# The start of a hybrid decoder step: u of the first 384 tokens from unnormed x, weights issued by two engines

## The reference

```
h = rmsnorm(x, norm1_w)                 # x * rsqrt(mean(x*x) + eps) * w
proj = h @ w_in                         # u, gates, xBC, dt, q, k, v, z
u = proj[..., OFF_U:OFF_Q]              # 512 columns, input of the S5 mixer
bu = einsum('bgph,...', b_bar, u)       # then a scan over time, y, GELU, GLU
gates = sigmoid(proj[..., OFF_GATE:])   # 24 tiles of 128 columns
```

## Time and profile before

| what | value |
|---|---|
| median of three runs | 1685.16 us (1684.84 to 1686.6) |
| span of the profiled execution | 1684.5 us |
| time of the profiled execution beside its span | none given; the span is its measure |
| TensorE busy | 1654.0 us |
| VectorE, ScalarE, GpSimd busy | 966.9, 556.0, 791.2 us |

### The profile page before, as it was taken

The page is one execution under the profiler, slowest core; times in us unless marked ns, Lnnn a source line. Parts: engine busy times, 40 slices in busy tenths (PEclk is TensorE's granted clock), DMA queues, the critical chain, the costliest instruction groups (busy, mean ns, idle before and its releaser), DMA issues. The chain is left out here.

```text
span 1684.5 us, 30884 instructions
## 1 busy us (share of the span) xinstructions
PE 1654.0 (98%) x12241; PEld 1604.7 (95%) x12241; DVE 966.9 (57%) x1642; ACT 556.0 (33%) x1240; POOL 791.2 (47%) x756
## 2 busy tenths in 40 slices
PE   7999999999999999999999999999999999999997
PEld 7999999999999998888899999999999999999997
DVE  6859811406634554778873289666665565744346
ACT  5332121342213332543411154443443333322233
POOL 5483122322221111141322325877777777787774
PEclk9999999999999999999999999999999999999998
DMA  5364363232233234434365431543433344966443
GB/s 209 84 127 133 104 203 98 89 92 91 87 93 103 89 130 134 161 115 140 126 218 191 152 126 42 180 162 145 151 141 141 141 167 165 367 224 267 162 187 103
DMA packets 95805, 245.85 MB, mean 146 GB/s; under 512 B 14369, under 2 KB 42273, under 8 KB 95417
## 3 DMA queue, kind: packets, MB, share of 16 engines
q1 hardware_dynamic: 73824, 174.48, 30.5%
q0 software_dynamic: 10256, 33.59, 6.7%
q10 hardware_dynamic: 11592, 35.96, 6.3%
HBM read 177.11 MB, written 66.65 MB: 145 GB/s over the span
## 5 line engine op out<-in xcount | busy, mean ns | idle before, releaser
L1642 PE MATMUL ps<-HL,WH 128*128 128x384 f32 (+1 forms) x1536 | 507.7, 331 | 4.4 <-DVE HL L691 1.8
L1643 PE MATMUL ps<-HH,WL 128*128 128x384 f32 (+1 forms) x1536 | 497.4, 324 | 0.0
L1644 PE MATMUL ps<-HH,WH 128*128 128x384 f32 (+1 forms) x1536 | 496.3, 323 | 0.0
L1642 PEld LDWEIGHTS ps<-HL,WH 128*128 128x128 f32 x1536 | 289.4, 188 | 15.6 <-issue 9.3
L1643 PEld LDWEIGHTS ps<-HH,WL 128*128 128x128 f32 x1536 | 289.7, 189 | 0.3
L1644 PEld LDWEIGHTS ps<-HH,WH 128*128 128x128 f32 x1536 | 289.6, 189 | 0.0
L1285 POOL TENSOR_TENSOR WL<-WRAW,WH 128x1024 fp32r<-128x1024 f32 x59 | 145.0, 2457 | 243.3 <-DMA WH<-in_w 243.3
L1282 POOL DMA_DIRECT2D WH<-in_w x59 | 34.6, 586 | 354.4 <-PE ps L1644 352.9
L2932 DVE TENSOR_TENSOR X<-X,ps 128x528 f32<-128x528 f32 (+2 forms) x170 | 107.9, 656 | 155.5 <-PE ps L2238 104.6
L2327 ACT ACTIVATE GT<-ps 128x384 f32<-128x384 f32 (+1 forms) x72 | 33.4, 465 | 215.5 <-PE ps L1644 183.5
L2932 DVE TENSOR_TENSOR RB<-RB,ps 128x528 f32<-128x528 f32 x60 | 42.1, 701 | 103.4 <-ACT RB L2847 85.9
(11 more groups left out here) (467 smaller groups left out, 4266.2 us busy)
## 6 DMA issues: line engine op xcount, KB each, us to landing
WRAW<-in_w SPq DMA_DIRECT2D x75, 512.0 KB, 3.4
ffn_scratch<-STG SPq DMA_DIRECT2D x70, 528.0 KB, 3.6
WH<-in_w POOLq DMA_DIRECT2D x62, 512.0 KB, 4.6
SOP<-ffn_scratch SPq DMA_DIRECT2D x36, 528.0 KB, 7.9
gate_scratch<-GT ACTq DMA_DIRECT2D x24, 528.0 KB, 3.2
PX<-gate_scratch ACTq DMA_DIRECT2D x22, 528.0 KB, 4.2
HL<-ffn_scratch SPq DMA_DIRECT2D x22, 528.0 KB, 10.4
RAWB<-in_w SPq DMA_DIRECT2D x10, 1024.0 KB, 6.2
```

The costliest lines, as they stand in the source:

```text
L1642: nc.tensor.matmul(out, wh, rl, start=start, stop=False)
L1643: nc.tensor.matmul(out, wl, rh, start=False, stop=False)
L1644: return nc.tensor.matmul(out, wh, rh, start=False, stop=stop)
```

## The change

In chunk 0, u is computed from x times the norm weight, without the root; the root is multiplied in when VectorE copies u out of the accumulators (evict_first_u_dve). ScalarE and VectorE split this plain x as it lands. Units 0 and 1 come in three transfers for both (256, 256 and 512 columns of each), issued by ScalarE behind the first parameters; their low parts, and those of units 2 to 5, are subtracted by VectorE instead of GpSimd. SyncE issues units 2 and 3 ahead of x of chunk 1, and the bias table after it. The squares of chunk 1 are made first, six on ScalarE and two on VectorE, then those of chunk 0 and 2, each set in buffers of its own. The order of roots is chunk 1, 0, 2, the order of splits 1, 2, 0: the normed h of chunk 0, which the gates need, is split last. Gate 0 is taken in the order of chunks 1, 2, 0; taps begin after gate(1, [0, 1]), and gate(2, [0]) stands ahead of stt_rows(0). ScalarE does gate(2, [0]) ahead of its stt_rows(0) as well, with high_weights(7) still ahead of both. All four stores of u are issued after the last split.

```diff
+    ROOT_ORDER = (1, 0, 2)
+    SPLIT_ORDER = (1, 2, 0)
+    PIECES = [slice(0, 256), slice(256, 512), slice(512, 1024)]
...
+    def x_plain_high_act(k):
+
+        nc.scalar.wait_ge(s_x[k], 16)
+        if k == 0:
+            nc.scalar.wait_ge(s_par, 16)
+        nc.scalar.mul(HH[:, k, 0:384], X0[:, k, 0:384], prm("norm1", k, 1)).then_inc(xp_hi, 1)
+
+    def x_plain_low_dve(k):
+
+        dve = nc.vector
+        dve.wait_ge(xp_hi, k + 1)
+        dve.scalar_tensor_tensor(HL[:, k, 0:384], X0[:, k, 0:384], prm("norm1", k, 1), HH[:, k, 0:384].bitcast(F32),
+                                 ALU.mult, ALU.subtract).then_inc(xp_lo, 1)
...
+    def x_first_squares_act(ks):
+
+        for k in ks:
+            nc.scalar.activation(SQ0[:, k, :], X0[:, k, 0:384], ACT.Square).then_inc(pq_done, 1)
...
+    def x_second_sum_dve():
+
+        dve, pairs = nc.vector, GT[:, 0:768].rearrange("p (k c) -> p k c", c=384)
+        dve.wait_ge(pq_done, 4)
+        dve.tensor_tensor(SQ[:, 0:2], SQ[:, 0:2], SQ[:, 2:4], ALU.add).then_inc(pq_used, 1)
+        dve.wait_ge(s_xc[1], 128)
+        dve.tensor_tensor(pairs, X0[:, 6:8, 384:768], X0[:, 6:8, 384:768], ALU.mult).then_inc(pq_used, 1)
+        dve.wait_ge(pq_used, 2)
+        dve.tensor_tensor(SQ[:, 0:2], SQ[:, 0:2], pairs, ALU.add).then_inc(pq_used, 1)
+        dve.wait_ge(pq_done, SECOND_BY_ACT)
+        dve.wait_ge(pq_used, 3)
+        dve.tensor_tensor(SQ[:, 0:2], SQ[:, 0:2], HF0[:], ALU.add).then_inc(pq_used, 1)
+        dve.wait_ge(pq_used, 4)
+        dve.tensor_tensor(ACC[:, 384:768], SQ[:, 0], SQ[:, 1], ALU.add).then_inc(pq_used, 1)
...
+    def evict_first_u_dve(j):
+
+        dve = nc.vector
+        dve.wait_ge(r0_ok, 1)
+        dve.wait_ge(acc_done[0], j + 1)
+        dve.tensor_tensor(as_steps(UF[:, j, :], 0, 3), as_blocks(u_bank(j, 0), 3), as_blocks(GT[:, 0:384], 3),
+                          ALU.mult).then_inc(acc_free[0], 1)
...
-        x_chunk(0)
+        x_chunk(0, [0])
+        x_chunk(0, [1])
+        x_chunk(0, [2, 3])
+        x_chunk(0, [4, 5, 6, 7])
+        first_weights(2)
+        first_weights(3)
+        x_chunk(1)
         sp.dma_start(HOT[:], io["hot"]).then_inc(s_hot, 16)
         sp.dma_start(RTAB[:], io["rtab"]).then_inc(s_hot, 16)
-        first_weights(0)
-        first_weights(1)
-        first_weights(2)
-        x_chunk(1, range(4))
-        x_chunk(1, range(4, KD))
-        first_weights(3)
         x_chunk(2)
...
-        split_halves()
-        u = 2
+        first_lows_counted()
+        s5_powers()
+        s5_rows()
+        s5_squarings(0)
+        gate_lows_counted()
+        s5_squarings(1)
...
             if n == 0 and j == 2:
-                pe.wait_ge(split_ok, 4)
+                pe.wait_ge(half_ok, 5)
+            elif n == 1 and j == 2:
+                pe.wait_ge(h_lo, KD)
+                pe.wait_ge(r0_ok, 1)
             elif n == 2:
                 pe.wait_ge(acc_free[0], j + 3 if j == 0 else 4)
-                if j == 2:
-                    pe.wait_ge(acc_free[1], 1)
-            elif n == 1 and j == 2:
-                pe.wait_ge(acc_free[0], 1)
-                pe.wait_ge(h_lo, 2 * KD)
             for k in range(KD):
                 if j == 0:
-                    pe.wait_ge(h_lo, KD * n + k + 1)
-                if j == 0 and n == 0 and k in (0, 4):
-                    pe.wait_ge(*((half_ok, 2) if k == 0 else (split_ok, 2)))
+                    pe.wait_ge(*((xp_lo, k + 1) if n == 0 else (h_lo, KD * (n - 1) + k + 1)))
+                if j == 0 and n == 0 and k in (0, 2, 4):
...
+                    pe.wait_ge(half_ok, k // 2 + 1)
...
-        x_first_sums_pe()
-        bias_by_distance(0)
-        bias_by_distance(1)
-        x_spread_pe(0)
         u_pair(0, 0)
-        pe.wait_ge(bias_ev, 2)
-        u_pair(2, 0, {1: lambda: x_sums_pe(1), 3: lambda: x_spread_pe(1)})
-        u_pair(0, 1)
-        u_pair(2, 1, {1: lambda: x_sums_pe(2), 3: lambda: x_spread_pe(2)})
+        u_pair(2, 0, {4: lambda: x_sums_pe(1), 6: lambda: x_spread_pe(1)})
+        u_pair(0, 1, {0: lambda: x_sums_pe(0), 3: lambda: x_spread_pe(0)})
+        u_pair(2, 1, {3: lambda: x_sums_pe(2), 4: lambda: bias_by_distance(0), 5: lambda: x_spread_pe(2),
+                      6: lambda: bias_by_distance(1)})
...
-        gate(0, [0, 1])
+        gate(0, [1, 2])
+        gate(0, [0], lambda n, k: pe.wait_ge(h_lo, 2 * KD + k + 1))
+        gate(1, [0, 1])
         taps(0)
-        gate(0, [2])
         taps(1)
-        gate(1, [0])
+        gate(1, [2])
         taps(2)
-        gate(1, [1])
         taps(3)
-        gate(1, [2])
+        gate(2, [0])
         stt_rows(0)
-        for n in range(3):
-            gate(2, [n])
-            stt_rows(n + 1)
+        stt_rows(1)
+        gate(2, [1])
+        stt_rows(2)
+        gate(2, [2])
+        stt_rows(3)
...
+        for q in range(3):
+            c = PIECES[q]
+            act.dma_start(WRAW[:, :, c], io["w"][0:2, :, c].rearrange("u p n -> p u n")).then_inc(s_piece[q], 16)
...
-        for k in range(0, KD, 2):
-            x_first_square(act, k)
+        x_plain_high_act(0)
+        high_piece(0)
+        x_plain_high_act(1)
+        act.wait_ge(ar_ok, 1)
+        nc.scalar.activation(SF("mag"), SF("ar"), ACT.Exp).then_inc(mag_ok, 1)
+        high_piece(1)
         nc.scalar.activation(SF("unused_root")[:, 0:1], ZERO[:], ACT.Sqrt)
-        high_half(0)
-        x_root_act(0)
-        high_half(1)
-        x_split_act(0, 2)
-        x_squares_act(1, range(2))
-        x_split_act(2, 3)
+        x_plain_high_act(2)
+        x_plain_high_act(3)
+        high_piece(2)
+        for k in range(4, KD):
+            x_plain_high_act(k)
         high_weights(2)
-        x_split_act(3, 4)
-        x_squares_act(1, range(2, 4))
-        x_split_act(4, 5)
         high_weights(3)
-        x_split_act(5, 6)
-        bias_rows(0)
-        x_split_act(6, 7)
-        bias_rows(1)
-        x_split_act(7, 8)
-        x_squares_act(1, range(4, KD))
+        x_squares_act(1, range(SECOND_BY_ACT))
+        x_first_squares_act(range(KD))
         x_root_act(1)
         act.wait_ge(red_ok, 1)
         nc.scalar.activation(SF("sin"), SF("r"), ACT.Sin)
         nc.scalar.activation(SF("cos"), SF("r2"), ACT.Sin).then_inc(sin_ok, 1)
-        x_squares_act(2, range(4))
-        x_split_act(8, 11)
-        evict_u(0, 0)
-        x_split_act(11, 13)
-        evict_u(1, 0)
-        x_split_act(13, 16)
-        x_squares_act(2, range(4, KD))
-        evict_u(2, 0)
-        evict_u(3, 0)
-        x_root_act(2)
+        nc.scalar.activation(SF("unused_root")[:, 0:1], ZERO[:], ACT.Sqrt)
+        for k in range(KD):
+            x_split_act(k, k + 1)
+            if k == 1:
+                x_root_act(0)
+            if k == 5:
+                x_root_copy_act()
+            x_squares_act(2, [k])
         evict_u(0, 1)
         evict_u(1, 1)
-        x_split_act(16, 24)
+        x_root_act(2)
+        x_split_act(8, 10)
+        bias_rows(0)
+        bias_rows(1)
+        x_split_act(10, 12)
         evict_u(2, 1)
+        x_split_act(12, 14)
         evict_u(3, 1)
+        x_split_act(14, 18)
+        high_weights(4)
+        evict_u(0, 2)
+        x_split_act(18, 19)
+        evict_u(1, 2)
+        x_split_act(19, 21)
+        high_weights(5)
+        x_split_act(21, 23)
+        evict_u(2, 2)
+        evict_u(3, 2)
+        x_split_act(23, 24)
         for j in range(4):
-            evict_u(j, 2)
-            if j == 1:
-                high_weights(4)
-                high_weights(5)
+            act.wait_ge(acc_free[0], j + 1)
             act.wait_ge(acc_free[2], j + 1)
             act.dma_start(uscr[j * P:(j + 1) * P, :], UF[:, j, :]).then_inc(s_ust, 16)
...
+        def low_piece(q):
+
+            c = PIECES[q]
+            dve.wait_ge(first_high, q + 1)
+            tt(WL[:, :, c], WRAW[:, :, c], WH[:, :, c].bitcast(F32), ALU.subtract).then_inc(half_ok, 1)
+
+        x_plain_low_dve(0)
+        low_piece(0)
+        x_plain_low_dve(1)
+        low_piece(1)
+        x_plain_low_dve(2)
+        x_plain_low_dve(3)
+        low_piece(2)
+        for k in range(4, KD):
+            x_plain_low_dve(k)
+        for u in (2, 3):
+            dve.wait_ge(first_high, u + 2)
+            tt(high_low(u)[1], WXR[:, u - 2, :], high_low(u)[0].bitcast(F32), ALU.subtract).then_inc(half_ok, 1)
         dve.wait_ge(den_ok, 1)
         nc.vector.reciprocal(SF("den"), SF("den")).then_inc(den_inv, 1)
-        x_split_dve(8, 16)
-        x_add_dve(2, range(KD))
+        x_second_sum_dve()
+        x_first_add_dve(0)
+        x_recip_dve(1)
+        x_first_add_dve(1)
+        x_first_add_dve(2)
+        x_split_dve(0, 3)
+        x_recip_dve(0)
+        x_split_dve(3, 8)
+        x_third_sum_dve()
+        for j in range(2):
+            evict_first_u_dve(j)
         x_recip_dve(2)
-        x_split_dve(16, 24)
+        for j in range(2, 4):
+            evict_first_u_dve(j)
+        x_split_dve(8, 18)
+        dve.wait_ge(first_high, 6)
```

(50 more changed lines are left out.)

178 lines of the change are left out of this document (73 added, 105 removed).

## The result

The changed kernel takes 1693.37 us (median, 1693.05 to 1696.03) against 1685.26 for the kernel before: a ratio of 1.0051, 95% interval 1.0036 to 1.0065. It is slower by 8.1 us, outside the range. The profiled execution took 1693.05 us, with a span of 1691.3, against a span of 1684.5 before.

A forecast was written before the change was run, and what follows sets the result against it. TensorE, busy 98% of the span, was taken as the bound, so only gaps could be saved: 10.5 us at the start, 3.0 left at the first gate, none after unit 7's landing; 1685.2, shifted to 1685.5 us, range 1680.8 to 1689.3.

The forecast's parts named there:

- The chain to the first gate: From the first product to the first gate: start 10.5 us earlier, first gate at 66.2 instead of 69.16, 3.0 left.
- the wait at the sums: At chunk 1's sums: TensorE comes at 22.4 and waits 3.4 us for the squares, until 25.8.
- the sentence on W: VectorE's W passes: 13.8 us uncontended, no term for GpSimd's subtractions, at most 2.1 us.
- The deciding step: Stores of u, then U loads at 78.5: unit 7 lands at 103.0, second transposes at 105.1, the 3.0 us gone.
- Rival A: Shorter chain to the stores of u, gaining 4.5 us to 1680.7; sign: stores out before 67.3; chance 0.29.
- Rival B: Clock at 1.2 GHz from 25.8 on, after the sums: 3.9 us slower, 1689.1; chance 0.22 with other store lateness.
- Rival C: Early start fails, TensorE starts at 12.8, 0.9 us late at chunk 1's sums: 1686.1; within the likeliest case, 0.49.
- the main sum: Start of TensorE at 6.8, first two k at the slow clock to 10.7, first pair ending at 17.2.
- term (d): Waiting at 22.4 may bring back 1.2 GHz: nothing to 2.1 us; small end taken, forecast shifted by 0.3.

The follow-up runs named there:

- e4: Changed kernel plus 36 never-read products of 384 columns on TensorE just ahead of the third gate; 1690.99 us, 1.0035.
- e2: Changed kernel with GpSimd's second set of squarings moved behind unit 6's subtraction and the third set behind unit 7's; 1684.93 us, 0.9997.
- e3: Changed kernel with unit 6's low part subtracted by VectorE instead of GpSimd, GpSimd's order otherwise kept; 1685.98 us, 1.0004.
- e5: Changed kernel with OFF_re and OFF_im set to zero, leaving out six two-operand VectorE passes; 1683.98 us, one execution.
- e8: On top of e2, ScalarE issues the first two weights' three transfers only after x's fourth tile has landed; 1691.64 us, 1.0037.
- e10: On top of e2, every small product of the taps issued twice with the same result; 1698.42 us, 1.0079.
- e9: On top of e6, ScalarE's stt_rows(0) ahead of its gate(2, [0]), and TensorE's taps groups set apart between gate chunks and transposes; 1684.24 us, 0.9992.
- e6: On top of e2, SyncE loads unit 7's weights together with unit 6's, ahead of the loads of U; 1687.35 us, 1.0008.
- e1: Changed kernel with GpSimd's second set of squarings run before it counts the low parts of units 4 and 5; 1696.53 us, 1.0052.
- e11: Kernel before the change, with only GpSimd's first two sets of squarings moved ahead of unit 6's subtraction; 1697.7 us, 1.0066.

## Why the prediction was wrong

**The chain to the first gate** held at every mark: first product 6.8 forecast and 7.06 measured, the wait for the first split of chunk 1 0.85 and 0.80, the ends of chunk 1's two pairs 42.6 and 52.9 against 41.76 and 53.27, first gate 66.2 against 66.37, start of W 71.3 against 71.31. Only the wait at the sums was 1.36 where I had 3.4: TensorE came at 23.4, a microsecond later than thought, and x a little sooner. That was idle either way.

**The step that failed** is the sentence on W: "these subtractions have moved to VectorE, so I take no such term". It is right for units 4 and 5, but unit 6's stays with GpSimd, and the change puts the second set of squarings ahead of it, as its diff shows. I had the row that shows the two engines holding each other up and used it in one direction only, as GpSimd slowing VectorE (4.4 instead of 2.3 us). In the other direction it costs GpSimd 1.95 us for an operation of 0.22. Then "TensorE, with the third gate's first chunk now ahead of the transposes, is there at ... 102.3" took the low part for ready. The term that I took as nothing measured +6.3 of wait and +2.4 of clock (e4), 8.7 in all, and e2 and e3 show that without it the time is 1684.9 to 1686.0, where the forecast was 1685.5.

The Trainium skill (SBUF — State Buffer, Who interferes with whom) says that VectorE's operation with two inputs in SBUF and a GpSimd operation that reads SBUF share a pair of ports under an exclusive lock, and that the loser blocks for the whole instruction. The trace agrees: 1.95 us is nearly one VectorE pass for each GpSimd operation, in e5 the pace returns when the passes end, and in e2 VectorE's pass at 79.83 is longer by nearly the whole of GpSimd's subtraction. By that rule, read ahead of time, the sets of squarings cost GpSimd one VectorE pass per operation as long as W lasts.

**The deciding step**, unit 7's landing at 103.0, was off by 3: the stores, forecast to land for the U loads by 78.5, did so by 77.06, and unit 7 landed 22.9 us after that, not 24.5, at 100.0. It was no bound in the changed kernel. In e3 it landed at 101.4 and ScalarE's copies were held as described, by the cast and then by the second gate's store until 102.9; the second transposes stood at 103.94 against my 105.1. The mechanism was right; its mark was 1.2 too late.

**Rival A** did not come true by its own sign: it wanted the stores out before 67.3, and they went out from 70.34 to 73.25, as the sum had them (70.7 to 72). The other half of it, unit 7 sooner, did come, by 3.0 us, and gave nothing, since the third gate, which stands ahead of the transposes, was held until 104.09. **Rival B** named the right mechanism, the clock, at the wrong place: at 24.74 the wait was 1.36 and the clock stayed whole; at 97.8 it was 6.33 and the clock fell. The Trainium skill (TensorE: Matmul & The Clock Gate, HAM oscillation) had told against the change with waits for data; what it describes is a long wait, and the trace agrees for the one of 6.33 us (e4 beside it). I had set it beside a wait at the sums of 3.4 us, which measured 1.36, and there the clock stayed whole.

**Rival C** was too kind: it priced a start at 12.8 at 0.9 us; e8, with 14.71, lost 6.1 at the first gate, where the same working gives 28.4 at the sums against 25.8, 2.6. From first product to sums TensorE took 15.7 us there (to 30.44), not the 13.7 of my working, which is thirteen k at the fast 1.05 and leaves out the slow start that I had counted in the main sum; and the sums to beat were at 24.26: 2.6+2.0+1.5 is the 6.1. By e8's 1.6 us of free start, one at 12.8 would cost 4.2 (an estimate). **Clock, term (d)**: the 0.57 between 386 and 390 us that I read as coming "after a stretch of small products, with no wait" stands behind eighteen products of 8 columns (383.56 to 385.6) and looks like what e10 makes on purpose; I weighed it for a wait and not for the taps, which the change puts in rows twice as long. It is not in every execution: of the thirteen profiles four have it there.

**Still open**: the 1.4 us that e9's lead of 2.6 loses in the late stages; why the granted clock is lower in e6 than in e2; and whether rows as long as the change's lower it.

## What to carry to other kernels

When a change moves work in one engine's queue, list everything queued behind it there, with what each signals and to whom (e1: the count also let SyncE's loads go; e2: eight microseconds for the place of one group). A slow-down between two engines in a trace is to be priced for both. A long wait of TensorE is to be costed with the clock behind it: here 6.3 us of wait cost 8.7. And before a difference of a microsecond or two is put down to an edit, the mean granted clocks of the executions are to be compared: e2's eleven lie at 1682.58 us with 0.997 to 1688.51 with 0.994.

## What the runs showed of the hardware

- GpSimd's operations of 16 columns, 0.22 us by themselves, took 1.95 us each while VectorE worked through two-operand passes of 2.3 us, and kept their 0.22 beside its memset of 1.76 us (e5, the two at 86.74); VectorE was held up by one longer GpSimd operation in turn (4.49 instead of 2.3 us for the pass at 79.83 in e2, beside the subtraction of 2.42).
- Beside a standstill of 6.33 us from 97.8 the clock was at 1.2 GHz from 99 to 109; beside waits of 1.36 and 0.8 us at 24 and 30 it was not. With the standstill filled with products (e4) it stayed at 2.4 GHz there. It fell beside the waits of 9.96 us in e1 (from 106) and 8.29 us in e11 (from 104) too.
- TensorE without a gap, but in products of 32 columns, fell to 1.2 GHz: in e10 at 92 and at 105, in rows of them from 86.8 to 95.6 and from 100.3 to 108.9. In the one profile with the taps in shorter rows (e9) it stayed at 2.4 GHz there.
- A kernel's executions differ in their mean granted clock, and their times with it: 0.994 to 0.997 and 1688.51 to 1682.58 us over eleven executions of e2.
